# A latent-attention kernel on one core: values of two heads formed at once, with the latent keys as the stationary operand

## What is computed

```
def mla_expand(ckv, kpe, w_ukv, k_hn):
    kvu = (ckv @ w_ukv).reshape(B, T, N_HEADS, QK_NOPE + V_DIM)
    k_nope, v = kvu[..., :QK_NOPE], kvu[..., QK_NOPE:]
    k_pe = jnp.broadcast_to(kpe[:, :, None, :], (B, T, N_HEADS, QK_ROPE))
    k = rms_norm(jnp.concatenate([k_nope, k_pe], axis=-1), k_hn)
    return k, v

s = jnp.einsum('bqhd,bkhd->bhqk', qblk, k).astype(jnp.float32) * scale
p = jax.nn.softmax(s, axis=-1).astype(v.dtype)
return jnp.einsum('bhqk,bkhd->bqhd', p, v)
```

## Time and profile before

| | |
|---|---|
| Runs, us | 1566.51, 1567.57, 1570.05 |
| Median, us | 1567.57 |
| Profiled execution, span from first to last instruction, us | 1566.4 |
| Its own device time, us | not listed apart from the span; the fastest run is 1566.51 |
| TensorE matmuls busy | 98% |
| TensorE weight loads busy | 95% |
| VectorE, ScalarE, GpSimd busy | 71%, 47%, 18% |
| Mean granted clock of TensorE | 0.995 of full speed |
| Attention heads on TensorE | from about 107 to 331 us |
| Matmuls, instructions in all | 10775, 26496 |

### The profile page before, as it was taken

How to read it: one execution, slowest core, us unless ns; L and a number is a source line. 1 busy time by engine, 2 the same in 40 slices (tenths; PEclk the granted TensorE clock), 3 DMA queues, 4 the chain that set the end, 5 groups by cost and what they waited for, 6 DMA issues and landing times.

```text
span 1566.4 us, 26496 instructions
## 1 busy us (share of the span) xinstructions
PE 1538.6 (98%) x10775; PEld 1483.5 (95%) x10775; DVE 1113.9 (71%) x1882; ACT 743.6 (47%) x1236; POOL 287.6 (18%) x344
## 2 busy tenths in 40 slices
PE   8989999999999999999999999999999999999998
PEld 6989788899999999999999899989999999999998
DVE  5657877866779746665467999988688468568453
ACT  3435555653544423442235766676365335335332
POOL 0010111000156524453253023221000000000000
PEclk9999999999999999999999999999999999999999
DMA  9332332132354544444333388875203222222322
GB/s 329 110 109 62 110 103 82 36 122 81 96 168 148 162 128 127 155 136 135 113 116 95 78 180 174 175 151 132 81 28 101 88 81 75 88 81 75 91 68 78
DMA packets 142464, 178.12 MB, mean 114 GB/s; under 512 B 13025, under 2 KB 121257, under 8 KB 141320
## 3 DMA queue, kind: packets, MB, share of 16 engines
q1 hardware_dynamic: 120128, 109.68, 22.3%
q0 software_dynamic: 21888, 66.66, 17.2%
q10 hardware_dynamic: 328, 0.10, 0.0%
HBM read 148.93 MB, written 2.79 MB: 97 GB/s over the span
## 4 chain that ended last, share of the span: by engine, by line
PE 87%; DVE 8%; ACT 2%; issue 1%; DMA 1%; POOL 0%; DVEq 0%; ACTq 0%
PE PS L777 23%; PE PS L779 22%; PE PS L782 22%; PE PS L858 5%; PE PS L860 5%; PE PS L859 5%; PE PS L1185 1%; PE PS L1196 1%; PE PS L1138 1%; DVE PTL L2698 1%; DMA MODA<-in_w_mod 1%; DVE WL L2099 0%; PE PS L1161 0%; DVE TMP L2288 0%; DVE X L2441 0%
## 5 line engine op out<-in xcount | busy, mean ns | idle before, releaser
L777 PE MATMUL PS<-HH,WH 128*128 128x320 f32 (+1 forms) x1168 | 269.6, 312 | 2.8 <-DVE HL L2299 2.2
L779 PE MATMUL PS<-HL,WH 128*128 128x320 f32 (+1 forms) x1168 | 266.1, 309 | 0.0
L782 PE MATMUL PS<-HH,WL 128*128 128x320 f32 (+1 forms) x1168 | 265.4, 308 | 0.0
L2425 DVE SCALAR_TENSOR_TENSOR X<-PS,MODV,X 128x128 f32<-128x128 f32 (+2 forms) x216 | 81.6, 434 | 185.4 <-PE PS L782 185.3
L777 PEld LDWEIGHTS PS<-HH,WH 128*128 128x128 f32 x1168 | 194.5, 188 | 7.5 <-issue 3.5
L779 PEld LDWEIGHTS PS<-HL,WH 128*128 128x128 f32 x1168 | 196.0, 188 | 0.0
L782 PEld LDWEIGHTS PS<-HH,WL 128*128 128x128 f32 x1168 | 195.8, 188 | 0.0
L2099 DVE TENSOR_TENSOR WL<-RAW,WH 128x2048 fp32r<-128x2048 f32 (+2 forms) x56 | 126.6, 2261 | 65.1 <-ACT WH L1503 64.9
L777 PE MATMUL PS<-HIDH,WH 128*128 128x320 f32 x704 | 163.0, 312 | 0.3 <-DVE HIDL L2356 0.3
L1867 ACT ACTIVATE BGW<-BGW,SC 128x512 f32<-128x512 f32 x112 | 80.8, 723 | 173.4 <-DVE BGACC L2247 124.0
L699 POOL TENSOR_TENSOR BGACC<-BGACC,BGW 128x512 f32<-128x512 f32 x97 | 132.4, 1365 | 159.8 <-ACT BGW L1867 158.6
(11 more groups left out here) (409 smaller groups left out, 3206.0 us busy)
## 6 DMA issues: line engine op xcount, KB each, us to landing
BGW<-in_w_mod POOLq DMA_DIRECT2D x112, 256.0 KB, 3.0
RAW<-in_ffn_w_gate SPq DMA_DIRECT2D x22, 1024.0 KB, 5.3
RAW<-in_ffn_w_up SPq DMA_DIRECT2D x22, 1024.0 KB, 5.4
MODA<-in_w_mod POOLq DMA_DIRECT2D x48, 256.0 KB, 3.7
RAW<-in_ffn_w_down SPq DMA_DIRECT2D x16, 768.0 KB, 4.7
RAW<-in_ffn_w_down SPq DMA_DIRECT2D x8, 1024.0 KB, 5.1
RAW<-in_conv_w_pw SPq DMA_DIRECT2D x16, 512.0 KB, 5.3
WL<-RAW POOLq DMA_DIRECT2D x8, 1024.0 KB, 9.8
```

What stands on the lines that cost most here:

```text
L777: mm(o, wh, xh, start=first, stop=False)
L779: mm(o, wh, xl, start=False, stop=False)
L782: ins = mm(o, wl, xh, start=False, stop=last)
L2425: ins = V.scalar_tensor_tensor(out=X[:, m, t:t + b - a], in0=tile2(n)[:, bank, a:b], scalar=g, in1=X[:, m, t:t + b - a], op0=ALU.mult, op1 ...
```

## The change

The values of heads h and h+1 (h even) are formed together, straight with keys along the partitions: the latent keys (CKH, CKL) are the stationary operand, 128 keys at a time, and 256 value columns of two heads the moving one. That is one block for two heads, two tiles (`va`, `vb`) of three key blocks each, 36 matmuls of 256 columns. `values_across`, VT, its copy and the six transposes are gone. The block stands where `values` stood, at the start and at the end of each odd head (for the even head that follows). VH is twice as wide, and VL is in two parts, one in the free half of an odd head's WH slot, one in new room of 5120 bytes; the slots of the modulation rows move. The value columns of both heads are in the even head's unit (1792 columns instead of 1536), and an odd head's unit has 768 instead of 1024. The rest of the diff is blank lines.

```diff
+ODD_HEAD = 768
...
-    o += [("dq", 2), "ctxout", ("dq", 3), ("kn", 0), ("stat", "cq"), ("pe", 0), ("vt", 0), ("rot", 0), ("qn", 0), ("v", 0)]
+    o += [("dq", 2), "ctxout", ("dq", 3), ("kn", 0), ("stat", "cq"), ("pe", 0), ("rot", 0), ("qn", 0), ("va", 0), ("vb", 0)]
...
-            o += [("kn", h + 1), ("qn", h + 1), *even(h + 1, "pe"), ("vt", h + 1)]
+            o += [("kn", h + 1), ("qn", h + 1), *even(h + 1, "pe")]
...
-            o += [("v", h + 1)] + (last[::-1] if h % 2 else last)
+            o += [*even(h + 1, "va"), *even(h + 1, "vb")] + (last[::-1] if h % 2 else last)
...
-        VH = sb("VH", [P, NKT, VD], R_HID + 38912, F32R)
-        VL = sb("VL", [P, NKT, VD], R_HID + 41984, F32R)
+        VH = sb("VH", [P, NKT, 2 * VD], R_HID + 38912, F32R)
-        VT = sb("VT", [P, KEYS], R_T[6])
...
+        R_SPARE = region(5120)
+        spare_half = (UNIT + ODD_HEAD) * 4
+        VL = [sb("VL0", [P, NKT // 2, 2 * VD], R_WH + spare_half, F32R), sb("VL1", [P, NKT // 2, 2 * VD], R_SPARE, F32R)]
+        moda_at = (R_WL + spare_half, R_WL + spare_half + 2048, R_WH + spare_half + 3072, R_SPARE + 3072)
+        MODA = [sb(f"MODA{i}", [P, 512], at) for i, at in enumerate(moda_at)]
...
-                 (lambda r, v=v: v(r, 512, KVT, 256), cols(w_ukv[0], h * 256))]
+                 (lambda r, v=v: v(r, 512, KVT, NOPE), cols(w_ukv[0], h * 256, NOPE))]
...
+                d += [(lambda r, v=v, i=i: v(r, ODD_HEAD, KVT, 2 * VD)[:, :, i * VD:(i + 1) * VD],
+                       cols(w_ukv[0], (h + i) * 256 + NOPE, VD)) for i in range(2)]
...
-            units.append((("head", h), 1536 if h % 2 == 0 else 1024, d))
+            units.append((("head", h), 1792 if h % 2 == 0 else ODD_HEAD, d))
...
-                "head": lambda n: ("vt" if n[1] else "qn", n[1]), "wo": lambda n: ("wo", n[1] + 1),
+                "head": lambda n: ("vb" if n[1] % 2 == 0 else "qn", n[1]) if n[1] < HEADS - 1 else ("o", n[1], 2), "wo": lambda n: ("wo", n[1] + 1),
```

The instructions of TensorE:

```diff
-            def values_across(h):
+            def values(h):
                 s = U[("head", h)] % 2
-                product(("vt", h), (WH[:, s, :], WL[:, s, :]), 512 + P, KVT, 256, CKH, CKL, n=KEYS // 2).then_inc(mm_done, 1)
-            def values(h):
-                ps = begin(("v", h))
-                was_read(pe, ("vt", h))
-                for t in range(NKT):
-                    ins = tr(flat(ps)[:, t * P:(t + 1) * P], VT[:, t * P:(t + 1) * P], EYE[:])
-                ins.then_inc(mm_done, 1)
+                for i, n in enumerate((("va", h), ("vb", h))):
+                    ps = flat(begin(n))
+                    for t in range(NKT // 2):
+                        out = ps[:, t * 2 * VD:(t + 1) * 2 * VD]
+                        at = slice((NKT // 2 * i + t) * P, (NKT // 2 * i + t + 1) * P)
+                        for k in range(KVT):
+                            w = slice(ODD_HEAD + k * 2 * VD, ODD_HEAD + (k + 1) * 2 * VD)
+                            mm(out, CKH[:, k, at], WH[:, s, w], start=k == 0, stop=False)
+                            mm(out, CKL[:, k, at], WH[:, s, w], start=False, stop=False)
+                            ins = mm(out, CKH[:, k, at], WL[:, s, w], start=False, stop=k == KVT - 1)
+                    ins.then_inc(mm_done, 1)
...
-            values_across(0)
...
-                    values_across(h + 1)
...
-                was_read(pe, ("v", h))
+                was_read(pe, ("va", h - h % 2))
+                was_read(pe, ("vb", h - h % 2))
...
-                    values(h + 1)
+                    if h % 2:
+                        values(h + 1)
```

The copies of ScalarE, whose calls change in the same way:

```diff
-                n = ("v", h)
-                filled(act, n)
-                A(VH[:].rearrange("p j v -> p (j v)"), flat(tile2(n))[:, 0:KEYS], ACT.Copy).then_inc(sem("v_hi"), 1)
+                for i, n in enumerate((("va", h), ("vb", h))):
+                    filled(act, n)
+                    part = VH[:, NKT // 2 * i:NKT // 2 * (i + 1), :].rearrange("p j v -> p (j v)")
+                    A(part, flat(tile2(n))[:, 0:KEYS], ACT.Copy).then_inc(sem("v_hi"), 1)
```

The low parts of VectorE, with the same `if h % 2` at the call:

```diff
-                V.tensor_tensor(line(VL[:]), flat(tile2(n))[:, 0:KEYS], line(VH[:]).bitcast(F32), ALU.subtract).then_inc(free_of(n), 1)
+                for i, n in enumerate((("va", h), ("vb", h))):
+                    dve.wait_ge(sem("v_hi"), h + i + 1)
+                    part = VH[:, NKT // 2 * i:NKT // 2 * (i + 1), :]
+                    V.tensor_tensor(line(VL[i][:]), flat(tile2(n))[:, 0:KEYS], line(part).bitcast(F32), ALU.subtract).then_inc(free_of(n), 1)
```

More of the change, by code:

```diff
@@ L258, in program @@
         MROW = sb("MROW", [P, 512], R_T[5])
-        MODA = [sb(f"MODA{i}", [P, 512], (R_WH, R_WL)[i // 2] + (i % 2 * UNIT + 1536) * 4) for i in range(ROW_SLOTS)]
         MROWA = sb("MROWA", [P, 512], R_HH + 7 * TOK * 4)
@@ L472, in program @@
             d = [(lambda r, v=v: v(r, 0, QLT, NOPE), cols(w_uq[0], h * QK, NOPE)),
-                 (lambda r, v=v: v(r, 512, KVT, 256), cols(w_ukv[0], h * 256))]
+                 (lambda r, v=v: v(r, 512, KVT, NOPE), cols(w_ukv[0], h * 256, NOPE))]
             if h % 2 == 0:
-                d += [(lambda r, v=v, i=i: v(r, 1024, QLT, P)[:, :, i * ROPE:(i + 1) * ROPE],
+                d += [(lambda r, v=v, i=i: v(r, ODD_HEAD, KVT, 2 * VD)[:, :, i * VD:(i + 1) * VD],
+                       cols(w_ukv[0], (h + i) * 256 + NOPE, VD)) for i in range(2)]
+                d += [(lambda r, v=v, i=i: v(r, 1280, QLT, P)[:, :, i * ROPE:(i + 1) * ROPE],
                        cols(w_uq[0], (h + i) * QK + NOPE, ROPE)) for i in range(2)]
-            units.append((("head", h), 1536 if h % 2 == 0 else 1024, d))
+            units.append((("head", h), 1792 if h % 2 == 0 else ODD_HEAD, d))
         for m in range(0, KT, 2):
@@ L1095, in rotary @@
                 s = U[("head", h)] % 2
-                product(("pe", h), (WH[:, s, :], WL[:, s, :]), 1024, QLT, P, CQH, CQL).then_inc(mm_done, 1)
+                product(("pe", h), (WH[:, s, :], WL[:, s, :]), 1280, QLT, P, CQH, CQL).then_inc(mm_done, 1)
             def keys(h):
@@ L1102, in keys @@
                     pe.wait_ge(sem("ck_ready"), KVT)
-                product(("kn", h), (WH[:, s, :], WL[:, s, :]), 512, KVT, 256, CKH, CKL, n=KEYS // 2).then_inc(mm_done, 1)
+                product(("kn", h), (WH[:, s, :], WL[:, s, :]), 512, KVT, NOPE, CKH, CKL, n=KEYS // 2).then_inc(mm_done, 1)
             def rotate_queries(h):
@@ L1201, in weighted @@
                 ps = begin(("o", h, g))
+                c = slice(h % 2 * VD, (h % 2 + 1) * VD)
+                value = lambda t: (VH[:, t, c], VL[t // (NKT // 2)][:, t % (NKT // 2), c])
                 if g == 0:
                     was_read(pe, ("pt", h, 0))
-                    split3([ps[:, 0, 0:P]], VH[:, 0, :], VL[:, 0, :], [(PTCH[:], PTCL[:])], True, True).then_inc(mm_done, 1)
+                    split3([ps[:, 0, 0:P]], *value(0), [(PTCH[:], PTCL[:])], True, True).then_inc(mm_done, 1)
                     return
@@ L1208, in weighted @@
                 for k in range(5):
-                    ins = split3([ps[:, 0, 0:256]], VH[:, k + 1, :], VL[:, k + 1, :],
+                    ins = split3([ps[:, 0, 0:256]], *value(k + 1),
                                  [(PTH[:, g - 1, k, :], PTL[:, g - 1, k, :])], k == 0, k == 4)
@@ L1676, in keys @@
                 A(keys2(KNH[:]), tile2(n)[:, :, 0:KEYS // 2], ACT.Copy).then_inc(sem("kn_hi"), 1)
-            def values_across(h):
-                n = ("vt", h)
-                filled(act, n)
-                A(keys2(VT[:]), tile2(n)[:, :, 0:KEYS // 2], ACT.Copy).then_inc(free_of(n), 1)
             def rotary_high(h):
@@ L1692, in values @@
             def values(h):
-                n = ("v", h)
-                filled(act, n)
-                A(VH[:].rearrange("p j v -> p (j v)"), flat(tile2(n))[:, 0:KEYS], ACT.Copy).then_inc(sem("v_hi"), 1)
+                for i, n in enumerate((("va", h), ("vb", h))):
+                    filled(act, n)
+                    part = VH[:, NKT // 2 * i:NKT // 2 * (i + 1), :].rearrange("p j v -> p (j v)")
+                    A(part, flat(tile2(n))[:, 0:KEYS], ACT.Copy).then_inc(sem("v_hi"), 1)
             def round_output(k):
                 if k < EARLY:
-                    filled(act, ("vt", HEADS - 1))
+                    filled(act, ("qn", HEADS - 1))
                 was_read(act, ("o", k, 2))
@@ L2623, in values @@
             def values(h):
-                n = ("v", h)
-                dve.wait_ge(sem("v_hi"), h + 1)
                 line = lambda r: r.rearrange("p j v -> p (j v)")
-                V.tensor_tensor(line(VL[:]), flat(tile2(n))[:, 0:KEYS], line(VH[:]).bitcast(F32), ALU.subtract).then_inc(free_of(n), 1)
+                for i, n in enumerate((("va", h), ("vb", h))):
+                    dve.wait_ge(sem("v_hi"), h + i + 1)
+                    part = VH[:, NKT // 2 * i:NKT // 2 * (i + 1), :]
```

(1 more changed line is left out.)

## The result

The changed kernel takes **1570.89 us** in the median of 21 runs (1567.73 to 1573.31), beside 1567.61 for the kernel before; the ratio is 1.0015 [1.0009, 1.0022]. By the ratio that is 2.4 us slower (the medians are 3.3 apart), inside the 0.2% that the prediction set as its bound for "same", and 0.9 us above the top of its range. A second set of runs gave 1.0012 [1.0001, 1.0022].

What follows compares the result with a forecast made beforehand. TensorE, busy 98%, was taken as the bound, with three other chains ending within a microsecond of its work. Even heads -2.4, odd +1.76, start +0.5 sum to -0.1: 1567.4 us; range 1562.2 to 1570.0, the forecast's own 1565.5 to 1569.2.

Steps and rivals of the forecast that it cites:

- TensorE's own work: All heads: 36 matmuls of 0.120 us, 4.33 a block; 16.9 + 5.7 go, 17.3 comes, 5.3 us less work.
- Rival D: Value block: each changed stationary operand costs its 0.188 us load, +9.8 us in all, 1577.2; chance 0.06.
- Even heads: Heads 2, 4, 6: sums start 0.8 us earlier, held by QNL; other savings become waits; 3 x -0.8 = -2.4 us.
- The DIAGL wait: Even heads, behind the weighted values: the 0.7 us of removed transposes becomes a wait on the low diagonals.
- Odd heads: Heads 1, 3, 5: block fills the modulation-row wait and sums come earlier; net +0.13, +0.70, +0.93, together +1.76 us.
- The start and head 0: Start and head 0: 3.0 later spread, less 1.7 of clock and 0.8 gained as in an even head, +0.5 us.
- Its first term: Start: the block ahead of the head sums moves the first spread from 109.03 to 112.0, +3.0 us.
- The gain behind it: Head 0, credited with the gain of an even head, 0.8 us.
- 1.7 is lost and 1.7 regained: Clock at the start: before loses 3.4 us at low clock; after, one 2.8 us hole loses 1.7, regaining 1.7.
- Rival C: Start: low clock comes twice, also behind the uncovered wait of some 1.8 us before the rotation; +1.7, 1569.1; chance 0.10.
- A: Whole change: all of TensorE's saving comes back, -5.3 us, 1562.3; chance 0.20.
- B: Start: the hole does not bring the low clock, another 1.7 us back, 1565.7; chance 0.10.

Runs made afterwards that it cites:

- values of odd heads cut: Kernel before without 10 of the 12 value matmuls of each odd head (1, 3, 5, 7); 1566.72 us, ratio 0.9995.
- the sums first: Changed kernel with head 0's sums and first modulation product ahead of the value block of heads 0 and 1; 1567.51 us, ratio 0.9993.
- the wait ahead of the rotation filled: Changed kernel with 12 matmuls of the keys' product put on TensorE ahead of rotation 0; 1569.98 us, ratio 1.0008.
- the weights later: Changed kernel with the next weight unit's rounding behind the third turned tile and its splitting behind the head's root; 1571.11 us, ratio 1.0016.
- the block cut: Changed kernel without 30 of the 36 block matmuls of heads 2, 4 and 6; 1564.60 us, ratio 0.9977.
- the two cuts: Kernel before without 10 of 12 value matmuls per odd head, 1566.72 us; changed kernel without 30 of 36 block matmuls in heads 2, 4, 6, 1564.60 us.
- the kernel before with the sums first: Kernel before with head 0's six value transposes moved behind the head sums and first modulation product; 1566.75 us, ratio 0.9990.
- the split block: Changed kernel, first half of head 0's block ahead of rotation 0, second behind sums and modulation product; 1565.50 us, ratio 0.9983; again 1564.56, 0.9977.

## Why the prediction was wrong

- **TensorE's own work.** The block costs what it said: 0.120 a matmul, 4.33 a block. Rival D, a weight load left open each time, did not happen.
- **Even heads, -0.8 each.** Right. The sums start 14.98 us behind the head's scores instead of 15.82, 0.84 earlier; heads 2, 4 and 6 changed by -0.29, -1.03 and -1.05, together -2.4 as predicted (-3.0 in the second trace). A wait on KNL that it did not name takes part of QNL's; in head 2 the MODA rows came late (1.99 at 197.51, 1.44 before). The DIAGL wait is there, 0.60.
- **Odd heads, +0.13, +0.70, +0.93.** Measured +0.20, +0.82, +1.03. The block fills the wait for MODA, 2.93 us before. Right, 0.3 short in all.
- **The start and head 0, +0.5.** This step failed. Its first term was right: the first spread moved from 19.92 to 22.97 in the trace without a low stretch ahead of it, +3.05 for +3.0. The gain behind it was 0.4 instead of 0.8 (from spread to head 1's scores 29.40 before, 27.31 after, 1.7 of it clock). The term that failed is the clock's: "1.7 is lost and 1.7 regained". Against the one trace of before it held: in the second trace of the changed kernel, which lost nothing ahead of the spread, the scores of head 7 start 225.06 us behind the first keys matmul, in before 225.09. But the runs of the same kernel put it 1.9 to 2.4 above. The 6.9 us at the low level had been read as a property of the kernel before and were one execution. The same start lost 1.7 with the values of odd heads cut (and 1.7 with the sums first, a changed order). The start of the changed kernel lost 1.7 behind its wait in three traces (twice as it is, once with the wait ahead of the rotation filled) and 3.4 in two (the weights later, the block cut). With either start it is 1.7 or 3.4; few as the traces are, they show no 1.7 that the change gives back.
- **Rival C**, left out of the forecast at 0.10, came on top in the first trace (24.57 instead of 22.97) and in two of the six traces with its wait.
- **The sum.** With no credit for the clock, the prediction's own terms give -0.1 + 1.7 = +1.6; with the 0.3 of the odd heads and the 0.4 of head 0 it is +2.3, beside +2.4 and +1.9 measured. The runs split this in two. At the same mean granted clock the span of the changed kernel is 1.5 to 1.8 us longer: 1568.8 (9 runs) beside 1567.2 (22) at 0.995, 1567.8 (6) beside 1566.3 (26) at 0.996, 1567.3 (7) beside 1565.5 (23) at 0.997. That is near the +1.6 that is left without the credit. And its clock was lower, not higher: 0.9954 in 33 runs, 0.9965 in the 111 runs of before, with a standard error of 0.0003; at some 0.7 us for each 0.001, the slope of the runs of before, that is another 0.8, an estimate. Side by side on one chip the difference was 0.9954 to 0.9961, not clear of noise, so its size stays open.
- **The rivals.** A, all TensorE's saving counts, fell to the two cuts: 0.8 of 7.0 us and 5 to 6 of 10.8. The rule of the Trainium skill that the prediction names for this rival ("Perfetto Trace Analysis", section "Identifying the Most-Contended Engine") points at TensorE, its weight loads busy 95%, as the engine to relieve first; what a microsecond taken from it is worth, these cuts show, depends on the place. B, a hole that brings no low clock, did not happen behind the 2.7 us wait in any of the six traces that have it. The range had its upper end at C plus 0.9; with the credit for the clock as an unknown of its own, 0 to 1.7, C would have reached 1570.8.

## What to carry to other kernels

When TensorE's work shrinks, ask at each edge which chain sets the next start; here one of 8.73 us that ends on VectorE made the even heads deaf to what TensorE did. A new block belongs where the engine waits anyway: the same 36 matmuls were worth +2.4 us in one piece ahead of the head sums and -2.7 us as two halves in the two waits, with the sums first; that order alone was worth -1.6 us to the kernel before (its interval reaches +0.2). A low-clock stretch read from one trace is a draw: count it with the chance it has, and take a second trace before crediting it.

## What had not been expected of the hardware

Four executions with a wait of exactly 1.88 us at the same instruction kept the granted clock at 1.00, two fell to 0.50 for about 3.4 us; nothing in the kernel differs between the two traces of the changed kernel. Every trace with a wait of 2.7 us ahead of the spread fell, three for about 3.4 us and three for about 6.8. The wait of 2.0 us near 825, by which the prediction judged the others, stands in all 15 traces; the low level follows in 13, not with the block cut and not in the kernel before with the sums first. Shorter waits can have it behind them as well: 0.91 and 0.60 in the split block (clock 0.50 in 134 to 136), 0.77 and 0.59 with the sums first (0.50 in 312 to 314). Of a lead gained in attention not all reaches the end each time: between the same two instructions of the convolution stage the split block's second trace took 176.8 us (883.83 to 1060.59), its first 175.4 (885.40 to 1060.75); why was not tried.
